# Banded attention of one core: the order of ScalarE's steps, the engine that splits three heads, and the place of the first output tiles

## The reference, cut to what matters

```
scores = einsum('bnqhgd,bnkhd->bnhgqk', qb, kb) * scale      # 128 queries x (own + previous 128 keys)
scores = where(mask, scores, -inf)                            # dist in [0, 128)
m = maximum(max(scores, -1), sink)
p = exp(scores - m)
denom = sum(p, -1) + exp(sink - m)
out = einsum('bnhgqk,bnkhd->bnqhgd', p / denom, vb)           # 8 heads of 64, 2 key heads
mix = concatenate([o_hg, o_att], axis=-1)                     # four recurrent heads of 128, then attention
h = h + mix @ w_out[l]                                        # 1024 x 1024 x 1024
```

## Time and profile before

| what | before |
|---|---|
| median of the runs (lowest) | 2974.66 us (2972.34) |
| the profiled execution, and its span | 2974.71 us, 2972.9 us |
| busy: TensorE / VectorE / ScalarE / GpSimd | 95% / 43% / 27% / 33% of the span |
| mean granted clock of TensorE | 0.976 of 2.4 GHz |
| the attention's units: M(0) to the first output tile | 432.31 to 523.86 us |

### The profile page before, as it was taken

One profiled execution on the slowest core, in us unless ns is written; L12 is line 12 of the kernel. 1 busy time (PEld: TensorE's weight loads), 2 busy tenths in 40 slices (PEclk: granted clock), 3 DMA queues, 4 the chain that ended last, 5 costly groups with the idle time before them and its releaser, 6 DMA issues.

```text
span 2972.9 us, 35148 instructions
## 1 busy us (share of the span) xinstructions
PE 2832.2 (95%) x13902; PEld 2313.4 (78%) x13902; DVE 1274.5 (43%) x1789; ACT 797.7 (27%) x1234; POOL 977.6 (33%) x1013
## 2 busy tenths in 40 slices
PE   8899987999999999998999999999979999999998
PEld 7888774788888888886897776787657888888886
DVE  4355537253333222245403444347566434443436
ACT  5344326231100011124113333234453111111114
POOL 3622311554333433323332110345124333333430
PEclk9999998999999999998999999999989999999999
DMA  5422230311121111024544232432012111111103
GB/s 215 154 88 100 100 119 3 128 57 57 42 68 45 42 56 42 29 43 96 115 113 100 86 107 75 161 126 100 29 43 99 42 48 50 42 42 42 56 29 113
DMA packets 156933, 230.59 MB, mean 78 GB/s; under 512 B 5284, under 2 KB 116239, under 8 KB 156823
## 3 DMA queue, kind: packets, MB, share of 16 engines
q1 hardware_dynamic: 110448, 136.85, 15.6%
q10 hardware_dynamic: 46375, 92.24, 8.8%
HBM read 181.33 MB, written 47.74 MB: 77 GB/s over the span
## 4 chain that ended last, share of the span: by engine, by line
PE 82%; DVE 10%; ACT 4%; issue 3%; DMA 1%; ACTq 0%; POOL 0%; DVEq 0%; POOLq 0%
PE PS L818 29%; PE PS L297 21%; PE PS L831 10%; PE PS L1156 4%; PE PS L2198 2%; PE PS L1162 2%; PE PS L845 2%; PE PS L1213 2%; PE PS L1843 2%; DVE SC L590 1%; PE PS L1913 1%; PE PS L1885 1%; PE PS L1901 1%; DVE SC L960 1%; DVE SC L963 1%
## 5 line engine op out<-in xcount | busy, mean ns | idle before, releaser
L2815 POOL CAST wh<-raw 128x512 fp32r<-128x512 f32 (+1 forms) x488 | 332.6, 696 | 1855.5 <-issue 1037.6
L2819 POOL TENSOR_TENSOR wl<-raw,wh 128x512 fp32r<-128x512 f32 (+1 forms) x488 | 659.8, 1362 | 0.0
L297 PE MATMUL PS<-UH,wh 128*128 128x512 f32 x1040 | 426.6, 410 | 37.2 <-DVE UL L680 16.3
L297 PE MATMUL PS<-UH,wl 128*128 128x512 f32 x1040 | 409.5, 394 | 0.0
L297 PE MATMUL PS<-UL,wh 128*128 128x512 f32 x1040 | 409.2, 394 | 0.0
L818 PE MATMUL PS<-UH,wh 128*128 128x512 f32 x1280 | 394.0, 389 | 0.0
L818 PE MATMUL PS<-UL,wh 128*128 128x512 f32 x1280 | 394.0, 389 | 0.0
L818 PE MATMUL PS<-UH,wl 128*128 128x512 f32 x1280 | 394.0, 389 | 0.0
L818 PEld LDWEIGHTS PS<-UL,wh 128*128 128x128 f32 x1280 | 240.2, 188 | 49.9
L818 PEld LDWEIGHTS PS<-UH,wh 128*128 128x128 f32 x1280 | 240.2, 188 | 49.9
L818 PEld LDWEIGHTS PS<-UH,wl 128*128 128x128 f32 x1280 | 240.2, 188 | 49.9
(11 more groups left out here) (326 smaller groups left out, 4014.7 us busy)
## 6 DMA issues: line engine op xcount, KB each, us to landing
raw<-in_w_up SPq DMA_DIRECT2D x33, 1024.0 KB, 7.1
raw<-in_w_in SPq DMA_DIRECT2D x27, 1024.0 KB, 9.8
raw<-in_w_down SPq DMA_DIRECT2D x22, 1024.0 KB, 4.9
raw<-in_w_gate SPq DMA_DIRECT2D x11, 1024.0 KB, 5.1
raw<-in_w_out SPq DMA_DIRECT2D x8, 1024.0 KB, 5.4
xres<-XT ACTq DMA_DIRECT2D x4, 2048.0 KB, 7.2
zgate<-SC ACTq DMA_DIRECT2D x32, 256.0 KB, 2.0
SC<-zgate ACTq DMA_DIRECT2D x16, 512.0 KB, 4.7
```

Of the source, the lines that this page charges most:

```text
L297: mm = pe.matmul(PS[:, banks[f], :], w[:, k, f * P:(f + 1) * P], u[:, k, half(h)], start=(k == 0 and j == 0), stop=(k == n_k - 1 and j == 2))
L2815: pool.tensor_copy(wh[slot][:, cols], raw[slot % 2][:, cols]).then_inc(hi_done[slot], 1)
L2819: low = pool.tensor_tensor(wl[slot][:, cols], raw[slot % 2][:, cols], wh[slot][:, cols].bitcast(F32), ALU.subtract)
```

## The change

The diff does three things.

1. In `First.scalar` the turned copy C(t-2) is issued before the exponentials P(t), not behind them: the order on ScalarE is now H(t-4), C(t-2), P(t).
2. `split_heads` on POOL is gone. ScalarE makes the high copy of heads 0, 1 and 2 at the end of steps 9, 11 and 13, and VectorE the low part at the end of steps 10, 12 and 14.
3. Output tiles J0, J1 and J2 are issued by `First.window` on TensorE at the ends of steps 16, 17 and 18: T(14), V(13), J0, T(15), V(14), J1, V(15), J2. They carry waits of their own: for all 16 maxima (J0, J1) or the last turned copy (J2), for the split heads, and for the attention's low parts of their tokens. `Join` now has `follows = True`, so no engine waits at its start for the other two; ScalarE waits for V(15) before it loads the residual.

```
--- before.py
+++ after.py
@@ -696,6 +696,9 @@
         class Join(Stage):
...
+            follows = True
+
             def __init__(self, name, first, segs, norm):
                 self.first, self.segs, self.norm = first, segs, norm
                 super().__init__(name)
@@ -707,24 +710,33 @@
                     for pos in range(2):
                         release(seg, pos, self.full, h * KT + 2 * pos + 2, 4)
 
+            def tile(self, pe, n):
+                first = self.first
+                h, t = n // KT, n % KT
+                seg, pos, i, f = self.segs[h], t // 2 % 2, t // 4, t % 2
+                slot = segments[seg][1][pos][0]
+                if f == 0:
+                    pe.wait_ge(w_ready[slot], use(seg, pos, i) + 2)
+                if n == 0:
+                    pe.wait_ge(*first.lo(1))
+                    pe.wait_ge(*first.o_lo(HG - 1))
+                if t == 0:
+                    pe.wait_ge(*first.wo_lo(16 if h else 12))
+                pe.wait_ge(*(self.free(n - 3) if n >= 4 else first.pt_done(16) if n >= 2 else first.mx(16)))
+                H, L = weights(slot, KT)
+                for k in range(KT):
+                    half_tiles(pe, H, L, (f,), k, KT, h, {f: n % 4}, self.full)
+                if n == KT + 1:
+                    self.norm.add_up(pe, 0, 0)
+
             def tensor(self, pe):
-                pe.wait_ge(*self.first.o_lo(HG - 1))
-                for n in range(2 * KT):
-                    h, t = n // KT, n % KT
-                    seg, pos, i, f = self.segs[h], t // 2 % 2, t // 4, t % 2
-                    slot = segments[seg][1][pos][0]
-                    if f == 0:
-                        pe.wait_ge(w_ready[slot], use(seg, pos, i) + 2)
-                    if n >= 4:
-                        pe.wait_ge(*self.free(n - 3))
-                    H, L = weights(slot, KT)
-                    for k in range(KT):
-                        half_tiles(pe, H, L, (f,), k, KT, h, {f: n % 4}, self.full)
-                    if n == KT + 1:
-                        self.norm.add_up(pe, 0, 0)
+                for n in range(3, 2 * KT):
+                    self.tile(pe, n)
 
             def scalar(self, act):
                 norm = self.norm
+                act.wait_ge(*self.first.wo_full(16))
+                act.wait_ge(*self.first.lo(1))
                 for h in range(2):
                     act.dma_start(XT[:, :, half(h)], xres.rearrange("(k p) t -> p k t", p=P)[:, :, half(h)]).then_inc(self.res[h].sem, 16)
                 for n in range(2 * KT):
@@ -1049,6 +1061,7 @@
                       ("a", 0, "in1_a", 0), ("a", 1, "in1_a", 1), ("kv", 0, "in1_kv", 0))
             AHEAD = 8
             STEPS = 9
+            HEADS_AT = (9, 11, 13)
 
             def __init__(self, name, enter):
                 self.enter = enter
@@ -1287,6 +1300,8 @@
                         turn(t - 2)
                     if 0 <= t - 3 < 16:
                         values(t - 3)
+                    if t >= 16:
+                        self.then.tile(pe, t - 16)
 
             def tensor(self, pe):
                 self.first_tiles(pe)
@@ -1517,24 +1532,19 @@
                 for t in range(16 + 4):
                     if 0 <= t - 4 < 16:
                         high(t - 4)
+                    if 0 <= t - 2 < 16:
+                        turned(t - 2)
                     if t < 16:
                         probs(t)
+                    if t in self.HEADS_AT:
+                        h = self.HEADS_AT.index(t)
+                        act.wait_ge(*self.o_loaded(16))
+                        act.activation(UH[:, h, :], ULf[:, h, :], ACT.Copy).then_inc(self.o_hi.sem, 1)
                     if t == 0:
                         act.wait_ge(*self.n2(HG))
                         act.activation(UH[:, last, :], self.o, ACT.Copy).then_inc(self.hi.sem, 1)
                         act.wait_ge(*self.o_stored(16 * last))
                         act.dma_start(ULf[:, 0:last, :], o1.rearrange("(k p) t -> p k t", p=P)).then_inc(self.o_loaded.sem, 16)
-                    if 0 <= t - 2 < 16:
-                        turned(t - 2)
-
-
-            def split_heads(self, pool):
-
-                pool.wait_ge(*self.o_loaded(16))
-                for h in range(HG - 1):
-                    pool.tensor_copy(UH[:, h, :], ULf[:, h, :]).then_inc(self.o_hi.sem, 1)
-                    pool.wait_ge(*self.o_hi(h + 1))
-                    pool.tensor_tensor(UL[:, h, :], ULf[:, h, :], UH[:, h, :].bitcast(F32), ALU.subtract).then_inc(self.o_lo.sem, 1)
 
             def columns(self, what, u):
                 return sm[:, what * 8 + (u % 2) * 4:what * 8 + (u % 2) * 4 + 4]
@@ -1709,6 +1719,10 @@
                         dve.tensor_tensor(UL[:, last, :], self.o, UH[:, last, :].bitcast(F32), ALU.subtract).then_inc(self.lo.sem, 1)
                     if 0 <= t - 4 < 16:
                         low(t - 4)
+                    if t - 1 in self.HEADS_AT:
+                        h = self.HEADS_AT.index(t - 1)
+                        dve.wait_ge(*self.o_hi(h + 1))
+                        dve.tensor_tensor(UL[:, h, :], ULf[:, h, :], UH[:, h, :].bitcast(F32), ALU.subtract).then_inc(self.o_lo.sem, 1)
 
         class Second(Stage):
 
@@ -2719,7 +2733,7 @@
         enter = Enter("enter")
         first = First("first", enter)
         norm_ffn1 = HalfNorm([("split", "norm_ffn_w")], ((4,), (5,)))
-        join = Join("out1", first, ("out1_a", "out1_b"), norm_ffn1)
+        join = first.then = Join("out1", first, ("out1_a", "out1_b"), norm_ffn1)
         final = HalfNorm([("scale", "final_norm_w"), ("split", "mix_pre_g_2")], ((0, 1), (3, 7)), store=True)
         FFN("ffn1", "ffn1", False, norm_ffn1, join.free(2 * KT), ((0, 0, 2),), final)
         second = Second("second", final)
@@ -2820,8 +2834,6 @@
                         low.then_inc(w_ready[slot], 1)
 
                 body(0, first=True)
-                if seg == "out1_a":
-                    first.split_heads(pool)
                 if iters > 1:
                     with nc.Fori(1, iters, engines=(pool.engine,), hint_back_edge=True) as i:
                         body(i)
```

## The result

The changed kernel takes 2956.22 us (median of five runs, 2951.77 to 2961.48). The kernel before, run beside it five times, has a median of 2977.48 us, which is 21.3 us more. One of those five runs took 4733.16 us; over the other four the median is 2976.07, which is 19.9 us more. The ratio, formed without that run, is 0.9929, with a 95% interval of 0.991 to 0.9948: 21 us less, between 15 and 27. Forecast were 2953.5 us and 21.2 us less. The median lies 0.2 us above the range of 2951 to 2956 and inside that of 2950 to 2961. The profiled executions differ by 22.6 us (2952.08 against 2974.71).

The account below looks back on a forecast made before the run. No engine was full; a chain of waits through ScalarE's order set the pace, with VectorE stretched beside POOL. Gains of 9.6 + 8.5 + 3.1 = 21.2 us took 2974.7 to 2953.5 us; forecast 2951 to 2956 (62%), wider range 2950 to 2961.

Parts of the forecast that it names:

- The pace: M(5) to M(15): VectorE becomes the bound at 3.57 us per unit; 39.1 us against 47.56, 8.5 gained.
- unit 8: Narrower unit between M(5) and M(15), left out of the forecast as under a us.
- the sum: Whole kernel: 9.6 + 8.5 + 3.1 = 21.2 us gained, from 2974.7 to 2953.5 us.
- The stretch beside POOL: M(2) to M(5): 10.05 us against 19.68, 9.6 gained, about 7 from VectorE operations stretched beside POOL, the rest part 1.
- The rule that would have left this work to the less busy GpSimd: Trainium skill's advice for saturated VectorE: head subtractions stay on POOL, losing 7 us less 3.4, some 2957.
- The tail: Behind M(15): J0 starts at 5.5 us, J2 ends at 25.1 where before 28.2; 3.1 us gained, barrier included.
- The clock: TensorE in the units: taken as 2.4 GHz; at 1.2 GHz TensorE sets the pace, 2.3 us more per unit.
- the first rival: A few units at 1.2 GHz, behind M(2) or where a head holds up VectorE: 4 us, 2957.5; 16%.
- The residual: Rival at J4: the residual's load comes late and costs 4 us, 2957.5; 7%.
- The order did quicken the units: Answers the rival that the swap does not quicken units: pace stays 4.76, only 12.7 us gained, 2962; 9%.
- Nothing was taken back later: Answers the rival that a later wait, hidden behind the present order, takes back the shift: 2972 to 2976; 3%.

Follow-up runs that it names:

- part 1 alone: Kernel before with only the turned copy ahead of the exponentials on ScalarE, heads on POOL, output tiles not moved; ratio to the kernel before 0.9955.
- part 2 undone: Changed kernel with POOL splitting heads 0 to 2 again, new order and moved tiles kept; ratio to the kernel before 0.9943.
- mended tail: Changed kernel with half the heads' subtractions put off, L(11) ahead of D(14), and J0 first in TensorE's reordered tail; median 2951.82 us, ratio 0.9915.
- tiles ahead of turns: Changed kernel with J0 issued ahead of T(14) and J1 ahead of T(15), both waiting for M(14) only; ratio to the kernel before 0.9941.
- POOL clears a tile: Changed kernel with POOL clearing one 128x1024 SBUF tile nine times once the heads land; one run, M(2) to M(5) 16.71 us.
- half heads alone: Changed kernel with only the second 512 tokens' subtractions of heads 0 to 2 put off to steps 17 to 19; ratio to the kernel before 0.9928.

## Why the prediction was right

**The pace.** The loop through ScalarE's order was the bound, and VectorE's own work became it. M(5) to M(15) gained 9.3 us, forecast 8.5. Without heads on VectorE ten units take 34.85 us, with them 38.24; forecast were 35.7 and 39.1. Most of the difference is unit 8, which was left out: the two steps that it makes narrower take 3.05 and 3.31 us. The three subtractions cost 3.39, forecast 3.4. About half of what the order gave here came by way of the clock (part 1 alone). That did the sum no harm, since it set VectorE's work against the 47.56 us as measured.

**The stretch beside POOL.** M(2) to M(5) fell by 9.65 us, forecast 9.6. Of these, 7.1 are the stretched operations up to M(4), which comes 6.47 us behind M(2) and not 13.59: forecast about 7. The other 2.5 lie between M(4) and M(5), and there the size was right and the cause was not. The step put them down to part 1, the order. They are the low clock of T(2), V(1) and S(5): with POOL at work they went in part 1 alone, where the clock was up, and stayed with part 2 undone, which has the new order too. The rule that would have left this work to the less busy GpSimd priced the part at 7 less 3.4; part 2 undone cost 6.3, the 2.5 of the clock included.

**The tail.** J0 came 5.41 us behind M(15), forecast 5.5, and J3 25.6, forecast 25.1: 2.7 us gained, not 3.1. The size was nearly right and the share was not: the step said that 3.1 us came from the tiles and the barrier. With the new order alone the first tile comes at 10.15 and not 11.81, and the tiles are worth 1.0 us behind M(15), in the changed kernel and alone. The step had half seen it (C(13) is no longer behind P(15)) and booked it to the wrong part. It also called L(11) older than J0 needs; it is made 3.6 us behind M(15), which T(14)'s own wait for D(14) hides, and which cost the experiment with early tiles its gain.

**The clock.** It was taken as 2.4 GHz, above 0.95 from 447 us on. S(3), from 446.33 to 448.4 us, still ran at the low clock (0.57 from 446 to 449); then it was 1.00 but for one dip (this window, and 0.81 in the next 3 us):

```profile
482.00:485.00 3.00, 3.00 (x17) 1.76 (x17) 2.86 (x17) 3.00 (x9) 0.00 (x0) 0.62 0.00 0
```

The dip follows 1.95 us of idle time behind the head's subtraction of 476.91 us. V(9) and S(13) at 1.2 GHz fitted into VectorE's next step, which holds a head too: S(13) ended 0.2 us before M(13) started. The changed kernel run again dips in the same place (0.50 from 482 to 485 us), with the same lengths. So the first rival, some units at the low clock where a head holds up VectorE, did happen in the changed kernel and cost nothing. Behind M(2) it happened in a relative of it (mended tail), where it cost 2.0 us and not 4.

**The other rivals.** The residual landed 8.3 us after issue, and J0's addition ended 1.8 us before J4. The order did quicken the units. Nothing was taken back later: the edited stretch gave 21.7 us and the ratio 21. The profiled pair differs by 1 us more, though M(2) starts 1.5 us later in the changed kernel; those differences lie outside of the edited stretch and I did not trace them.

**The sum.** The three terms came out at 9.65, 9.3 and 2.7 us where 9.6, 8.5 and 3.1 were forecast. That the total is within half a us is partly luck: the pace gave 0.8 more and the tail 0.4 less. The parts nearly add up as well: 16.9, 3.8 and 1.3 us alone are 22.0, together 21.7. That is partly luck too. Undone one at a time they are 16.7, 6.3 and 1.0, and the 2.5 us of the clock behind M(4) count with the order in the first set and with the heads in the second. Apart from them, the heads cost 1.3 us on ScalarE's old loop and 3.4 on VectorE in the new one.

## What to carry to other kernels

When no engine is full and the chain of waits runs round through four of them, walk each engine's order over two steps: one instruction that stands behind a longer one without needing it (a copy of 0.9 us behind 2.05 us of exponentials) was worth up to 17 of the 22 us. When the loop runs through TensorE, look at the clock of the pieces on it: by the estimates above about half of those 17 us were matmuls on the path at the low clock, and one profile of each kernel does not tell how often such a piece gets it. Before work is given to GpSimd because it idles, look at what VectorE does in that stretch: four in-place scalings of 1.14 us took 1.93 to 5.96 us beside it. When a tail is filled with tiles, list all inputs of the first tile with the time each is made; a tile put first in the queue holds up what stands behind it, and the gap ahead of it can cost the clock.

## What the runs showed of the hardware

- A write of POOL alone, without a read, stretches VectorE's in-place scalings from 1.14 to 3.49 and 4.08 us (POOL clears a tile).
- The length of TensorE's gap did not by itself decide its clock. Behind 2.59 us idle the clock stayed at 1.00 (changed kernel, T(14)); behind 2.05 us it fell to 0.51 (half heads alone), behind 3.2 to 0.54 (tiles ahead of turns), behind 1.12 it stayed (mended tail, J0). The kernel before and part 1 alone ran T(1), V(0) and S(4) in the same 1.97, 1.12 and 2.09 us and then idled for 1.59 and 1.60 us; T(2) took 1.97 us in the one and 1.09 in the other. An edit that shortened VectorE's steps by 1.6 us lost all of it in TensorE's tail (half heads alone). What decides between such gaps is not shown here.
